# Pairs of projection tiles in seven block products, and one root for fifteen tiles

## The reference

```python
def project(h, pos, W):          # h = RMSNorm(x), 544 tokens x 1024 features
    z = h @ W['w_in']
    qa, ka, va, qb, kvb, gb, gm = split(z)
    qa = rope(rmsnorm(heads(qa), W['g_qa']), pos)     # heads of 64 features
    ka = rope(rmsnorm(heads(ka), W['g_ka']), pos)
    qb = rope(rmsnorm(heads(qb), W['g_qb']), pos)
    keys = rope(rmsnorm(kvb[:, :, :, 0], W['g_kb']), pos)
    ...
def mem_kv(mem, W):              # 256 memory tokens
    kv = (rmsnorm(mem, W['g_mem']) @ W['w_mkv'])
    return stack([rmsnorm(kv[:, :, 0], W['g_mk']), kv[:, :, 1]])
```

## Time and profile before

| | us |
|---|---|
| median of 3 runs | 1269.58 (1269.3 to 1269.73) |
| profiled execution, from the first to the last instruction | 1270.2 |
| PE busy | 1242.2 |
| DVE busy | 668.9 |
| ACT busy | 363.6 |
| POOL busy | 204.0 |
| first tile's first matmul | 6.74 |
| first memory key matmul | 144.16 |
| first scores of the prompt stage | 221.58 |

### The profile page before, as it was taken

One profiled execution on the slowest core, in us unless ns is written; L12 is line 12 of the kernel. 1 busy time (PEld: TensorE's weight loads), 2 busy tenths in 40 slices (PEclk: granted clock), 3 DMA queues, 4 the chain that ended last, 5 costly groups with the idle time before them and its releaser, 6 DMA issues.

```text
span 1270.2 us, 19608 instructions
## 1 busy us (share of the span) xinstructions
PE 1242.2 (98%) x6934; PEld 979.2 (77%) x6934; DVE 668.9 (53%) x1517; ACT 363.6 (29%) x743; POOL 204.0 (16%) x396
## 2 busy tenths in 40 slices
PE   7999999999999999999999999999999999999999
PEld 6788765887877766766788887687888888888887
DVE  3776612585555525124135643339878788873331
ACT  4766741444444422112100015321121212110000
POOL 1000000433334425124000110131000101000000
PEclk9999999899999999999999999999999999999999
DMA  6342314423322689899292311022222222312240
GB/s 227 122 163 67 141 47 178 154 71 98 101 68 86 225 289 353 311 325 333 68 402 96 133 61 40 26 74 70 80 84 83 84 83 83 121 54 92 92 157 18
DMA packets 80868, 170.17 MB, mean 134 GB/s; under 512 B 10529, under 2 KB 48354, under 8 KB 79874
## 3 DMA queue, kind: packets, MB, share of 16 engines
q1 hardware_dynamic: 62962, 110.94, 26.1%
q10 hardware_dynamic: 13648, 47.49, 10.0%
q0 software_dynamic: 4160, 10.49, 2.5%
HBM read 159.07 MB, written 9.81 MB: 133 GB/s over the span
## 4 chain that ended last, share of the span: by engine, by line
PE 91%; DVE 4%; ACT 2%; issue 2%; DMA 1%; POOL 0%; ACTq 0%; DVEq 0%; SPq 0%; POOLq 0%
PE ps L2544 19%; PE ps L2581 11%; PE ps L2323 10%; PE ps L1617 9%; PE ps L491 9%; PE ps L1085 6%; PE ps L2356 4%; PE ps L546 3%; PE ps L1018 2%; PE ps L990 2%; PE ps L1004 2%; PE ps L473 1%; PE ps L2404 1%; PE ps L494 1%; PE ps L531 1%
## 5 line engine op out<-in xcount | busy, mean ns | idle before, releaser
L2544 PE MATMUL ps<-arena 128*128 128x272 f32 x1120 | 257.1, 392 | 0.8 <-DVE arena L2883 0.8
L2544 PEld LDWEIGHTS ps<-arena 128*128 128x128 f32 x1120 | 212.7, 190 | 45.1 <-DVE arena L2883 1.2
L491 PE MATMUL ps<-arena 128*128 128x272 f32 x512 | 122.9, 399 | 6.7 <-DVE arena L606 6.7
L1617 PE MATMUL ps<-arena 128*128 128x272 f32 x512 | 121.8, 395 | 0.5 <-PE ps L1717 0.5
L2581 PE MATMUL ps<-arena 128*128 128x272 f32 x528 | 121.8, 392 | 0.0
L491 PEld LDWEIGHTS ps<-arena 128*128 128x128 f32 x512 | 98.9, 194 | 27.4 <-issue 6.7
L1617 PEld LDWEIGHTS ps<-arena 128*128 128x128 f32 x512 | 95.8, 190 | 26.9 <-issue 8.4
L2581 PEld LDWEIGHTS ps<-arena 128*128 128x128 f32 x528 | 100.3, 190 | 20.7
L1085 PEld LDWEIGHTS ps<-arena 128*128 128x128 f32 x768 | 90.3, 196 | 11.9 <-issue 11.4
L1085 PE MATMUL ps<-arena 128*128 128x128 f32 (+1 forms) x768 | 95.9, 283 | 1.8 <-DVE arena L1212 1.8
L2271 ACT ACTIVATE arena<-arena 128x560 f32<-128x560 f32 x44 | 35.3, 848 | 159.2 <-DVE arena L2898 152.5
(11 more groups left out here) (374 smaller groups left out, 1736.7 us busy)
## 6 DMA issues: line engine op xcount, KB each, us to landing
arena<-in_w_close SPq DMA_DIRECT2D x68, 512.0 KB, 3.5
arena<-in_pages_cmp SPq DMA_DIRECT2D x128, 128.0 KB, 2.2
arena<-in_past_va ACTq DMA_DIRECT2D x6, 2048.0 KB, 11.9
arena<-in_w_down SPq DMA_DIRECT2D x16, 704.0 KB, 6.0
arena<-in_past_ka ACTq DMA_DIRECT2D x6, 1792.0 KB, 11.1
arena<-in_w_close ACTq DMA_DIRECT2D x16, 512.0 KB, 6.3
arena<-in_w_proj SPq DMA_DIRECT2D x15, 512.0 KB, 3.4
arena<-in_pages_ks SPq DMA_DIRECT2D x96, 64.0 KB, 4.2
```

Of the source, the lines that this page charges most:

```text
L491: last = pe.matmul(ps[:, 2 * (j % 2) + a, 0:HALF], w, h[:, k, a * HALF:(a + 1) * HALF], start=(k == 0), stop=(k == KD - 1))
L1617: last_one = pe.matmul(ps[:, gate_bank(q), 0:HALF], ring[:, n % CLOSE_RING, k * P:(k + 1) * P], m.h[:, k, half * HALF:(half + 1) * HALF], ...
L2544: last = pe.matmul(ps[:, bank(f, i), 0:HALF], w[:, k * P:(k + 1) * P], halved[:, rhs, k, :], start=(k == 0), stop=(k == 3))
```

## The change

- Tiles 0 and 1 stay. Tiles 2 to 15 are taken as seven pairs. With the features (k) and the tokens each cut in two halves, and the two tiles of a pair as the two rows of a 2x2 block matrix, a pair takes seven products of four matmuls (Winograd's form of Strassen's scheme): x1, y, x2, z1, x3, z2, x4. x1 to x4 are accumulated in one bank (banks 0 and 1 in turn) and ACT copies its state after each of the first three (`keep`); y has bank 2, z1 and z2 bank 3; DVE adds the pieces to `raw` (`put`).
- POOL makes four differences of h (`turn`, each 128x1088) once and four sums of weights per pair (`half_sums`, each 128x512).
- The gain of a head moves from ACT's copy into DVE's rotation. ACT squares `raw` in SBUF into one of four buffers.
- Head sums: PE multiplies the squares of up to four tiles with `pick_head`, 32 output lanes each, in four lane groups of the same two banks (`square_sums`). They are issued in pairs 1, 3, 5 and inside tile 16; all accumulate, so that each head of the 15 tiles has one lane.
- One root (`z`) is taken for all 15 tiles. SP writes it to DRAM (`kept_roots`) and reads it back with 30 transfers, each of which spreads one row over 64 partitions. DVE multiplies tiles 1 to 8 behind the sample values and tiles 9 to 15 behind the next block (`finish_tiles`).
- `spread` uses the space of w1, so SP loads w1 only behind the stores of `o_z` and `o_mk`.

```diff
@@ SP
         for j in range(1, NJOB):
-            if j >= RING:
-                sp.wait_ge(z_full, j - RING + 1)
+            before = j - RING
+            if before in (0, 1):
+                sp.wait_ge(z_full, full("tile", before))
+            elif before >= 2:
+                p, second = divmod(before - 2, 2)
+                sp.wait_ge(z_full, full("x4" if second else "y", p))
+                sp.wait_ge(pool_made, pooled("s", p, S4))
...
+        sp.wait_ge(x_root_ready, 2)
+        sp.dma_start(kept_roots[:, :], root).then_inc(const_in, 16)
+        sp.wait_ge(const_in, 16 * 8)
+        for j in range(1, NTILE):
+            for e in range(2):
+                src = kept_roots[place(j) + e:place(j) + e + 1, :].broadcast_to([HD, NT])
+                sp.dma_start(spread[j - 1][HD * e:HD * e + HD, :], src).then_inc(g_in if j <= 8 else mem_in, 16)
@@ POOL
+        def turn(to, a, b, after=None):
+            if after is not None:
+                pool.wait_ge(pool_made, pooled("t", after))
+            pool.tensor_tensor(turned[:, to], a, b, ALU.subtract).then_inc(pool_made, 1)
+
+        def half_sums(p):
...
+            for j in (a, b):
+                pool.wait_ge(chunk_in[j % RING], 16 * (j // RING + 1))
+            if p >= 1:
+                pool.wait_ge(z_full, full("z1", p - 1))
+            pool.tensor_tensor(half_sum[:, S1], w21, w22, ALU.add).then_inc(pool_made, 1)
+            pool.wait_ge(pool_made, pooled("s", p, S1))
+            pool.tensor_tensor(half_sum[:, S2], half_sum[:, S1], w11, ALU.subtract).then_inc(pool_made, 1)
+            if p >= 1:
+                pool.wait_ge(z_full, full("x3", p - 1))
+            pool.tensor_tensor(half_sum[:, S3], w11, w21, ALU.subtract).then_inc(pool_made, 1)
+            if p >= 1:
+                pool.wait_ge(z_full, full("z2", p - 1))
+            pool.wait_ge(pool_made, pooled("s", p, S2))
+            pool.tensor_tensor(half_sum[:, S4], w12, half_sum[:, S2], ALU.subtract).then_inc(pool_made, 1)
+
+        pool.wait_ge(h_ready, KD)
+        pool.wait_ge(squared, KD)
+        turn(T1, b12, b11)
+        turn(T2, b22, turned[:, T1], T1)
+        turn(T3, b22, b12)
+        turn(T4, b21, turned[:, T2], T2)
+        half_sums(0)
         for k in range(1, KD):
...
+        for p in range(1, NPAIR):
+            half_sums(p)
@@ ACT
+        def pair(p):
+            a, b = in_pair(p)
+            rs = ROOTS.get(("pair", p), ())
+            if p >= 1:
+                act.wait_ge(summed, made("12", p - 1))
+            keep("x2", p, p % 2, one_2)
+            keep("z1", p, Z_BANK, one_4)
+            logs(rs)
+            keep("x3", p, p % 2, one_3)
+            guesses(rs)
+            act.wait_ge(summed, made("12", p))
...
+            act.activation(squares[a % 4][:, :], raw[:, 0, :], ACT.Square).then_inc(z_out, 1)
+            if p + 1 < NPAIR:
+                keep_first(p + 1)
+            act.wait_ge(roped, b - 2)
+            keep("x4", p, p % 2, raw[:, 1, 0:HALF])
...
+            act.activation(squares[b % 4][:, :], raw[:, 1, :], ACT.Square).then_inc(z_out, 1)
@@ PE
+        def square_sums(i):
+            js = [j for j in range(4 * i, 4 * i + 4) if j >= 1]
+            pe.wait_ge(z_out, js[-1] + 1)
...
+            for a in range(2):
+                for j in js:
+                    c = 32 * (j % 4)
+                    last = pe.matmul(ps[c:c + 32, 4 + a, 0:HALF], pick_head[:, 6 - 2 * i:38 - 2 * i],
+                                     squares[j % 4][:, a * HALF:(a + 1) * HALF], start=(i == 0 or j == 4), stop=(i == 3))
             last.then_inc(sum_full, 1)
...
+        def pair(p):
+            a, b = in_pair(p)
+            if p >= 1:
+                pe.wait_ge(summed, made("11", p - 1))
+            part(Y_BANK, of_ring(a, 4), b21, True)
+            if p == 1:
+                pe.wait_ge(z_out, 2)
+            for r in ROOTS.get(("pair", p), ()):
+                sums(r)
+            pe.wait_ge(pool_made, pooled("s", p, S2))
+            pe.wait_ge(squared, kept("x1", p))
+            part(p % 2, of_sum(S2), turned[:, T2], False)
+            if p >= 1:
+                pe.wait_ge(summed, made("12", p - 1))
+            part(Z_BANK, of_sum(S1), turned[:, T1], True)
+            if ("pair", p) in SQUARES:
+                square_sums(SQUARES["pair", p])
+            pe.wait_ge(pool_made, pooled("s", p, S3))
+            pe.wait_ge(squared, kept("x2", p))
+            part(p % 2, of_sum(S3), turned[:, T3], False)
+            pe.wait_ge(pool_made, pooled("s", p, S4))
+            pe.wait_ge(squared, kept("z1", p))
+            part(Z_BANK, of_sum(S4), b22, False)
+            if p + 1 < NPAIR:
+                first_part(p + 1)
+            pe.wait_ge(chunk_in[b % RING], 16 * (b // RING + 1))
+            pe.wait_ge(squared, kept("x3", p))
+            part(p % 2, of_ring(b, 4), turned[:, T4], False)
@@ DVE
+        def pair(p):
+            a, b = in_pair(p)
+            if p == 1:
+                refined("x", x_root[:, :])
...
+            rope(b - 2)
...
+            put("11", p, raw[:, 0, 0:HALF], ps[:, Y_BANK, 0:HALF], one_1[:, p % 2])
+            for r in ROOTS.get(("pair", p), ()):
+                mean_of(r)
...
+            put("22", p, raw[:, 1, HALF:NT], one_3, one_4)
+            dve.wait_ge(z_full, full("z2", p))
+            put("12", p, raw[:, 0, HALF:NT], ps[:, Z_BANK, 0:HALF], one_2)
+            rope(a)
@@ SP in attend_prompt
-        sp.dma_start(w1, d["w_cmp1"]).then_inc(w_in, 16)
...
-        sp.wait_ge(m.z_full, m.NJOB)
+        sp.wait_ge(m.z_full, m.products_done)
         load_pages(0)
         m.store_tiles(sp)
+        sp.dma_start(w1, d["w_cmp1"]).then_inc(w_in, 16)
```

More of the change, by code:

```diff
@@ L301, in project @@
     MEMV, SAMPLE, VAL, NVAL = (0, 1), 2, 3, 3 + QT
-    WORK = [("tile", j) for j in range(NTILE)]
+    WORK = [("tile", 0), ("tile", 1)] + [("pair", p) for p in range(NPAIR)]
     for i in range(MH):
@@ L490, in product @@
                     for a in range(2):
[L491 removed]
+                        last = pe.matmul(z_pair(j)[:, a, :], w, h[:, k, a * HALF:(a + 1) * HALF],
                                          start=(k == 0), stop=(k == KD - 1))
@@ L495, in product, with part @@
                                      start=(k == 0), stop=(k == KD - 1))
-                if k == (3 if 2 < j < NTILE else KD - 2):
-                    for r in ROOTS.get(("tile", j), ()):
-                        sums(r)
+                if j == NTILE and k == KD - 2:
+                    square_sums(SQUARES["tile", NTILE])
             last.then_inc(z_full, 1)
+        def part(bank, w, rhs, begins):
+            for k in range(4):
+                last = pe.matmul(ps[:, bank, 0:HALF], w(k), rhs[:, k, :], start=(begins and k == 0), stop=(k == 3),
+                                 skip_group_check=not begins)
+            last.then_inc(z_full, 1)
@@ L552, in on_pe @@
         for kind, n in WORK:
-            product(n) if kind == "tile" else values(n)
-            if (kind, n) == ("tile", 3):
+            if kind == "pair":
+                pair(n)
+            else:
+                product(n) if kind == "tile" else values(n)
+            if (kind, n) == ("tile", 1):
+                first_part(0)
+            if (kind, n) == ("pair", 1):
                 columns()
@@ L580, in refined, with finish_tiles @@
             step.wait()
-            step.done(dve.scalar_tensor_tensor(out=out, in0=bend[:, n], scalar=1.5, in1=y,
-                                               op0=ALU.add, op1=ALU.mult))
+            step.done(dve.scalar_tensor_tensor(out=out, in0=bend[:, n], scalar=1.5, in1=y, op0=ALU.add, op1=ALU.mult))
+            step.wait()
+        def finish_tiles(js):
+            for j in js:
+                z = m.z[:, order[j], :]
+                dve.wait_ge(g_in, 16 * (1 + 16)) if j <= 8 else dve.wait_ge(mem_in, 16 * (1 + 14))
+                dve.wait_ge(roped, j)
+                dve.tensor_tensor(z, z, spread[j - 1][:, :], ALU.mult).then_inc(tile_done, 1)
@@ L614, in on_dve @@
         for w in WORK:
+            if w[0] == "pair":
+                pair(w[1])
+                continue
+            if w == ("tile", NTILE):
+                rope(NTILE - 1)
             for r in ROOTS.get(w, ()):
                 mean_of(r)
-            for r in ROOTS.get(w, ()):
-                if r != "x" and r != "mem" and r < NTILE:
-                    rope(r)
             if w == ("value", SAMPLE):
                 sample_values()
+                finish_tiles(range(1, 9))
+            if w == ("value", SAMPLE + 1):
+                finish_tiles(range(9, NTILE))
```

264 lines of the change are left out of this document (178 added, 86 removed).

## The result

The changed kernel takes **1255.17 us** (median of 4 executions, 1253.22 to 1257.63); beside it the kernel before took 1269.65 (1269.3 to 1270.43). The ratio is 0.9872 with a 95% interval of 0.9853 to 0.9891: 14.5 us less, where 18 were forecast. The time lies inside the range, 3.7 us above the point.

What follows compares the result with a forecast made beforehand. TensorE, busy 98% of the span, was taken as the bound: 12.83 + 9.3 + 1.5 - 5.1 - 0.6 = 18.0 us less. From 1269.58 that gives 1251.6, stated as 1251.5 us, range 1245.5 to 1260.

Steps and rivals of the forecast that it cites:

- Products: PE in the seven pairs: 28 matmuls fewer at 0.458 us each, 12.83 us less.
- Head sums: PE: 60 records, 13.75 us, become four bundles in lane groups, 1.11 us each, 4.4 in all; 9.3 us less.
- Rival 4: PE's head sums: lane groups don't run together for 32-lane sums; 9.3 us more, 1260.9 us; chance 4%.
- Waits that go: PE among the first tiles: waits of 0.9 and 0.6 us leave with the early head sums; 1.5 us less.
- The first stall: PE before pair 0's S2 x T2: POOL, slowed by DVE, has S2 at 30.9 us; 2.2 us idle.
- Rival 3: Start of the pairs: POOL and DVE's exclusion costs PE little, stalls 0.6 us, total 1247; chance 8%.
- The later stalls: PE in pair 1: S2 0.8 us late, x4 waits 2.1 us behind ACT's logarithm; nothing waits from pair 2 on.
- Tile 16: End of the pairs: tile 16 waits for the copy of pair 6's x4 out of bank 0; 0.6 us.
- Transfers: SP's queue: 30 broadcasts hidden, w1 lands at 216.2 us at the latest, needed at 222.44; cover 6 us or more, cost zero.
- rival 5: The 30 broadcasts hold SP's queue, w1 lands late: PE waits from 0.8 us each, slower above 1.4; 3% (partial: 5%).
- The base and the clock: Whole kernel: 0.6 us between span 1270.2 and median 1269.58 stays; one half-clock stretch kept, each more costs 3.4 us.
- Rival 1: Start: stalls 7.3 instead of 5.1 us plus one or two half-clock stretches; 1257 us, 1254.9 to 1260.5; chance 30%.

Runs made afterwards that it cites:

- b_eighth: The changed kernel with an eighth product of four matmuls per pair, y computed twice into a bank overwritten next; 1261.62 us, ratio to before 0.9922.
- c_full_lanes: The changed kernel with each head sum written over all 128 lanes, so a half's four matmuls run one after another; 1263.74 us, ratio to before 0.9935.
- d_dve_turns: The changed kernel with the four differences of h made on DVE behind its sum of squares, leaving POOL the half sums; 1250.76 us, ratio to before 0.9835.
- e_late: The changed kernel with two further differences of h on POOL ahead of the four that are used; 1262.72 us, ratio to before 0.9916.
- g_best: d_dve_turns with the memory mean's logarithm behind the copy in pair 1 and the first memory key tile in the other bank; 1248.95 us, ratio to before 0.9825.
- f_twice: The changed kernel with each of the 30 broadcasts followed by a second into an unread DRAM buffer; 1275.66 us, ratio to before 1.0018.
- h_pad: The changed kernel with the four narrow one-column products on TensorE repeated 14 times more; 1254.39 us, ratio to before 0.9861.
- a_same: The changed kernel unaltered, run in more executions; 1255.88 us, ratio to before 0.9874.

## Why the prediction was right, and where it was off

**Products.** Right: 12.83 us, with b_eighth as the test. The beat of a pair is 12.93 us here (25.86 for two), 0.1 more than the 12.84 of the earlier trace rows; with sums on 128 lanes in c_full_lanes it is 12.83, so the rest belongs to the bundles.

**Head sums.** Right in kind: a bundle takes 1.06 us against 1.11, but 0.2 more at the products around it, which the sum did not have: 8.7 us less, not 9.3. Why a change between 128 and 32 output lanes costs 0.1 us is open. Rival 4 had 3.67 and is refuted by c_full_lanes beside it.

**Waits that go.** The 0.9 and 0.6 us went. The first wait of all rose from 6.74 to 7.18, 0.4 us that I had not priced; it is 6.77 to 7.18 in the nine profiles of changed kernels, so part of it is spread.

**The first stall.** Forecast: S2 at 30.9, TensorE at 28.8, 2.2 us. Measured: S2's half sum ends at 31.03 (29.40 + 1.63), TensorE had finished at 29.1 to 29.3, 1.81 us. The mechanism is as told: the last three of DVE's seven adds met POOL, as the prediction had it, and took 8.92 us together where four before them took 3.20. It did not matter for DVE, since nobody waits for the sum of x so early. POOL paid as well: its first difference took 2.49 us, the others 2.88 to 3.00, and the two half sums 1.74 and 1.63 against 1.26 alone. At the prices alone, 4 x 2.49 and 2 x 1.26, S2 would have been ready at 16.28 + 12.5 = 28.8, before TensorE came; so POOL's plain speed does not explain the stall, and the 2.3 us of exclusion do. That the number came out so close is partly luck: POOL began at 16.28, not at 14.95, because ACT's squares ended 1.2 us later, while exclusion and semaphores cost it 2.3 us and not the 3.5 (2.8 + 0.7) of the prediction. The rule of the Trainium skill, "SBUF — State Buffer", section "Who interferes with whom", that a pair of ports is shared under an exclusive lock and a DVE instruction with two SBUF inputs contends for it with a GpSimd instruction that reads SBUF, agrees with the three adds of 2.83 to 3.03 us, each as long as a difference of POOL's and more, that took 0.72 alone. d_dve_turns shows where the stall came from, e_late that its length is paid in full. Rival 3, exclusion that costs little, falls.

**The later stalls.** Too large: the wait for S2 of pair 1, 0.8 us, is not there, and that behind ACT's logarithm is 0.5, not 2.1. The memory mean is taken at 54.7 us, not at 56.4 as I had it from the schedule laid out by hand. Together 2.3 us of stalls in place of 5.1. Pairs 2 to 6 have none, as forecast.

**Tile 16.** 0.58 us, forecast 0.6; g_best removes it by the other bank.

**The stage in sum.** Forecast 18.0. Gone: 12.83 + 9.65 + 1.53 = 24.0 up to the memory keys (14 head sums of 0.917 less three bundles there). Added: 1.81 + 0.50 + 0.58 + 0.44, and 0.6 around three bundles. 20.1 are left by this sum and 20.0 in the trace; the fourth bundle is 0.3 dearer than the single sum that stood there, so 19.6 at line 1279, where the forecast was 18.0 (its terms add up to 17.9). The stalls in pair 1, 2.9 us forecast and 0.5 measured, are the term of this sum that was mis-sized.

**Transfers.** Right in kind: hidden. The issues took 0.635 us, between the 0.52 and 0.79 of the earlier trace rows; the weights landed at 194.5 against 196.2 forecast at the latest (216.2 less 20.0), 8.3 us of cover against 6 or more. The point at which TensorE begins to wait would be 0.635 + 8.3 / 30 = 0.91 us a transfer, forecast 0.8. f_twice puts 0.64 x 2 = 1.27 there and makes TensorE wait. What rival 5 missed is the clock (11 us of half-clock stretch with TensorE back at work, beside a wait of 12.2): at 1.27 us a transfer the gain is already gone, where the prediction had the point at 1.4. The estimate from "SBUF — State Buffer" of the Trainium skill, section "Door 1: The DMA port swizzle", 0.71 us for a row over 64 partitions, is too long: the transfers were issued every 0.635 us and landed 2.9 to 3.5 us later, the last no more than 0.6 us slower than the first. At 0.71 each the last would have fallen 2 us behind, so the measurement decides; how far under 0.635 one would go, the run doesn't tell, since SyncE's queue sets that interval.

**From the stage to the whole.** Of 19.6 us at 203 us, 16.9 to 17.5 are left in span times clock (1266.4 less 1249.5 and 1248.9). The two profiled executions say the same: 1270.2 less 3.4 (the stretch of the earlier trace rows) and 1251.5 less 1.7 (3.4 us at half clock from 411.8) are 17.0 apart. 2.1 is the gap at line 1962, which no step of mine could have seen and h_pad shows. About 0.5 are two waits of the next stage, 0.3 and 0.2 us, which the kernel before did not have in its profile, where TensorE ran at half clock in that place and the others caught up. 19.6 less these is 17.0, so no term of size is without a cause. That 17.0 lies so near the 18.0 of the sum is luck in part: the stage gave 1.6 us more than forecast, and 2.6 that nobody had forecast went behind it.

**The base and the clock.** This is the step that was off most. I set the profiled execution, 1270.2 us, against the median of 1269.58 and took the 0.6 us between them as fixed. But an execution's time is 1.7 us more than its span, so the profiled one, with 3.4 us lost to the clock, belonged to 1271.9, and the median to spans near 1267.9, which in the later runs go with a mean clock of 0.999. That is about 1.7 us lost: the profile after, at 0.999, has one stretch of 3.4 us at half clock. The median of the changed kernel lies between executions of 0.996 and 0.997, 1253.5 x 0.0035 = 4.4 us lost. These 2.7 us are most of the 3.7 by which the forecast was low; the other 1.0 is 18.0 forecast against 17.0. Rival 1 had the further stretch and thereby the time (1254.9 with one), but for its first part, more stalls, it was wrong. The sum would have missed by 1.0 us at an equal clock; the clock, which the prediction said it couldn't place, made the rest. Whether the changed kernel draws half-clock stretches more often than the one before is not settled: both have them in some executions and not in others (before 0.993 to 0.999 in 25 executions, the changed kernel 0.995 to 0.999 in 8), and behind the same idle.

## What to carry to other kernels

Fewer matmuls are worth their beat exactly, when TensorE is busy 98% of the span; what decides the rest is whether the helpers' first operands are ready, and there the queue that makes them is to be chosen by where its work meets another engine's: four differences on POOL beside DVE's adds cost 1.8 us of TensorE, on DVE behind them, where one takes 1.28 us and not 2.49, nothing. Work that is hidden today should be given its cover in us and the point from which it isn't, since an uncovered wait costs more than its length when the clock falls behind it. The profiled execution must be set against the median through its own device time and its own clock, before a term is subtracted.

## What the runs showed of the hardware

- Matmuls with 32 output lanes in four lane groups run together: 16 records in 1.06 us, 3.67 on 128 lanes. Each such bundle costs the products around it 0.2 us (25.86 against 25.66 for two pairs between bundles).
- Whether a half-clock stretch follows an idle, and how long it is, differs between executions. The idle of 1.87 us in the next stage had 6.8 us behind it in the kernel before, 3.4 in a_same, e_late and h_pad, none in the changed kernel's own profile and in b_eighth. The idle of 2.63 us ahead of 411 us, which every kernel has, had none in four profiles (before, c_full_lanes, d_dve_turns, h_pad), 3.4 in two (after, b_eighth), 6.8 in two (a_same, e_late) and 10.2 in two (f_twice, g_best). Around the idle of 8.25 us it was 10.2, around that of 12.2 us 30.7, 22 of them with TensorE back at work.
- A half-clock stretch costs less than half its length where other engines are just behind TensorE: the 0.5 us wait in pair 1 is gone in a_same, that of 1.87 us is 0.4 in f_twice.
- A gap of 0.9 to 1.5 us on TensorE can come and go with 56 tiny matmuls added 450 us earlier in its queue.
- DVE and POOL both pay for operations of two SBUF inputs that overlap, DVE more: an add of 544 columns on DVE took 2.83 to 3.03 us beside POOL's differences and 0.72 alone, a difference on POOL 2.49 and then 2.88 to 3.00, a half sum on POOL 1.26 us alone (35.16 in e_late) and 1.6 to 1.75 beside DVE.
